# Tile 0's gate product computed among tile 1's expert rows, with its weights loaded twice

## The chip, the cores and the metric

The kernel runs on one core of a Trainium2 chip. The metric is the device time of one execution in microseconds (us). The engines are PE (TensorE), DVE (VectorE), ACT (ScalarE), POOL (GpSimd) and SP (SyncE, which here only issues weight loads); they run their own instruction lists and meet at semaphores.

## The reference, cut to what matters

Two layers follow one another on x of 256 tokens by 2048. The first ends with an expert lookup (each token takes 128 rows of `expert_u` and 128 rows of `expert_v`, each 2048 long) and a gated embedding; the second begins with a norm and a wide product.

```python
h = h + peer(rms_norm(h, ffn_norm_gain[i]), w_pq[i], sub_k1[i], sub_k2[i], expert_u[i], expert_v[i])
gate = jax.nn.sigmoid(rms_norm(h, ple_norm_gain[i]) @ w_ple_gate[i])
h = h + gate * (p[i] @ w_ple_proj[i])
...
h = rms_norm_2(x, norm_g)
proj = h @ w_in
```

The changed part is the line of `gate` and the sum behind it: a 256 x 2048 by 2048 x 2048 product, a sigmoid, and a sum into h.

## The kernel before, in words

Tokens lie in two tiles of 128 partitions (t = 0, 1); `h[:, t, :]` is the running sum. All large weights come as chunks of 128 x 2048 float32 (1 MiB): a chunk holds 512 rows of the weight by 512 columns, as four pieces k. A chunk c goes through five steps. SP loads it into one of the buffers `raw`. ACT's `split(c)` copies it to `whi` in a rounded format (signal `hi_done`). DVE's `split(c)` writes the rest, raw minus whi, to `wlo` (`lo_done`). PE multiplies: for each tile, eight products with `whi` (with the high part `xh` and the low part `xl` of the transposed input, four pieces each, signal `hi_used`) and four with `wlo` (`used`). `whi` and `wlo` have two buffers each, so ACT's copy of chunk c waits for `hi_used` and `lo_done` of chunk c-2, DVE's for `used` of c-2. SP loads c once `lo_done` of the chunk that had its `raw` buffer is there: two buffers while expert rows are gathered (`TWO_RAW`), four after.

`block_step` (L352) is one chunk's step on PE. Four chunks make a block of 512 output columns. The gate has 16 chunks (from `C_GATE`), four blocks n = 0 to 3.

Ahead of the gate are the expert rows. For pick i (0 to 127 belong to tile 0, 128 to 255 to tile 1), POOL gathers row u(i) and row v(i) for 128 tokens by an indirect DMA, 1 MiB each, in the order `ROW_ORDER`: u(i+8), then v(i). Eight or so buffers turn (`slots`; some lie in `xT`, in `raw` and in `whi`/`wlo`). DVE's `row_step` takes the dot product of u with the normed token, ACT makes a diagonal matrix of the weight, up to eight picks ahead of PE, and PE's loop over `PICKS` multiplies v by it (L774). In this loop stand also the second half of the query projection (chunks of its own, at picks 6 to 58), the embedding's projection (picks 86 and 92) and, for tile 0 alone, the turning of h into `xh`/`xl` (`gate_turn` on PE, `gate_entry` on ACT and DVE, at picks 160 to 188). Of tile 0's h nothing changes after DVE's pick 140 until the gate.

After the last row: DVE adds tile 1's sums into h (`peer_in`), PE turns tile 1, takes chunk 0 of the gate in parts (`gate_part`: tile 0 first, then tile 1), and then runs 15 `block_step`s with both tiles. The row norm is applied at the end, as the sigmoid's scale: ACT squares h's rows (`square_rows`, L984), DVE takes the mean, ACT the root (L988), DVE the reciprocal (`row_rstd`), and only then the first sigmoid (L1286) can run. Each block ends with ACT's sigmoids and DVE's product with `proj` and sum into h (L2043, L2046). In the last block the entry of the next norm (`entry(E_NORM2, ...)`, PE L396, ACT L975, DVE L1453) follows each chunk. The second layer's first stage, `in2_step`, comes next and uses both tiles. The order on each engine is written out by hand.

## Time and profile before

| | us |
|---|---|
| median of 3 runs (2412.11 to 2415.28) | 2414.21 |
| profiled execution, its own time | 2414.64 |
| its span | 2413.3 |
| granted TensorE clock, mean | 0.99 |
| PE busy | 2103.3 (87%) |
| DVE busy | 1402.8 (58%) |
| ACT busy | 650.9 (27%) |
| moved by DMA | 751.23 MB, mean 311 GB/s |

Times in all rows are us from the start of the span. Busy shares are averages over stages that have different limits, so a stage is read by itself: who is busy all of it, and what ended the waits of the others. In a row of the timeline, "x16" counts merged instructions, and the bracket at the end gives the idle time ahead of the group and who ended it.

### The profile page before, as it was taken

The numbers are of one execution on the slowest core, as the hardware profiler recorded it, in microseconds if no ns is written. First come the engines' busy times: TensorE is split into PE (matmuls) and PEld (weight loads), VectorE is DVE, ScalarE is ACT, GpSimd is POOL, SyncE is SP. The second block draws the span as 40 slices with busy tenths as digits, with TensorE's granted clock in tenths as the row PEclk, the third lists the DMA queues.
The fourth block names the chain that finished last, engine by engine and source line by source line (L and its number), as shares of the span: only waits on it lengthen the run. The fifth ranks groups of instructions, "written<-read, shape, count | busy, mean of one in ns | idle before, by whom it ended". The sixth has DMA issues, their size and how long they took to land.

```text
span 2413.3 us, 19575 instructions
## 1 busy us (share of the span) xinstructions
PE 2103.3 (87%) x7564; PEld 1348.0 (56%) x7564; DVE 1402.8 (58%) x1841; ACT 650.9 (27%) x923; POOL 666.7 (28%) x523
## 2 busy tenths in 40 slices
PE   8999979888887877777777777779999999999999
PEld 7887854444432433222332222227888888888887
DVE  4586685667586678444454444446557555744454
ACT  5464521111111110100010000005534443643332
POOL 0000144545455555554444444430000000000000
PEclk9999989999999999999999999999999999999999
DMA  7443489999999999999999999995455545455554
GB/s 285 158 173 124 157 340 420 413 422 421 421 421 421 421 422 414 422 421 421 422 422 421 421 422 421 421 407 222 175 208 179 198 174 175 160 195 194 189 180 147
DMA packets 105356, 751.23 MB, mean 311 GB/s; under 512 B 11952, under 2 KB 11952, under 8 KB 14384
## 3 DMA queue, kind: packets, MB, share of 16 engines
q0 software_dynamic: 73728, 536.90, 53.5%
q1 hardware_dynamic: 29520, 207.89, 23.9%
q10 hardware_dynamic: 2016, 5.18, 0.6%
q8 instruction: 60, 0.98, 0.2%
q14 instruction: 32, 0.26, 0.0%
HBM read 747.84 MB, written 2.10 MB: 311 GB/s over the span
## 4 chain that ended last, share of the span: by engine, by line
PE 56%; DMA 35%; DVE 4%; issue 2%; POOL 2%; ACT 1%; SPq 0%; ACTq 0%; POOLq 0%; DVEq 0%
PE ps L362 39%; DMA W<-in_expert_v,idx 26%; PE ps L774 12%; DMA raw<-in_expert_u,idx 3%; DMA wlo_row<-in_expert_v,idx 2%; DMA raw<-in_expert_v,idx 1%; DMA xT_rows<-in_expert_u,idx 1%; PE ps L396 1%; POOL W L313 1%; DMA W<-in_expert_u,idx 1%; DVE xT_rows L1854 1%; POOL xT_rows L313 0%; PE ps L662 0%; PE ps L661 0%; DVE raw L1854 0%
## 5 line engine op out<-in xcount | busy, mean ns | idle before, releaser
L362 PE MATMUL ps<-whi,xT 128*128 128x512 f32 x2560 | 616.2, 393 | 4.7 <-DVE xT L1453 2.0
L1442 DVE TENSOR_TENSOR wlo<-raw,whi 128x2048 fp32r<-128x2048 f32 x194 | 442.8, 2288 | 258.0 <-ACT whi L963 256.9
L774 PE MATMUL ps<-W 128*128 128x512 f32 x1008 | 465.3, 604 | 143.8 <-DMA W<-in_expert_v,idx 136.6
L362 PEld LDWEIGHTS ps<-whi,xT 128*128 128x128 f32 x2560 | 480.2, 189 | 105.7 <-DVE xT L1453 2.5
L963 ACT ACTIVATE whi<-raw 128x2048 fp32r<-128x2048 f32 x193 | 368.4, 1915 | 450.3 <-PE ps L362 256.6
L1854 DVE CUSTOM_DVE_ANT_0 W<-W 128x2048 f32<-128x2048 f32 x127 | 291.2, 2293 | 284.4 <-DMA W<-in_expert_u,idx 284.2
L774 PEld LDWEIGHTS ps<-W 128*128 128x128 f32 x1008 | 183.3, 191 | 415.3 <-issue 405.3
L362 PE MATMUL ps<-wlo,xT 128*128 128x512 f32 x1280 | 318.1, 391 | 7.4 <-DVE wlo L1442 7.4
L774 PE MATMUL ps<-raw,W 128*128 128x512 f32 x536 | 247.2, 604 | 71.0 <-DMA raw<-in_expert_v,idx 45.7
L362 PEld LDWEIGHTS ps<-wlo,xT 128*128 128x128 f32 x1280 | 241.3, 189 | 57.9 <-DVE wlo L1442 7.8
L313 POOL DMA_INDIRECT W<-in_expert_v,idx x129 | 185.1, 1435 | 259.9 <-PE ps L774 243.9
L1854 DVE CUSTOM_DVE_ANT_0 raw<-raw,W 128x2048 f32<-128x2048 f32 x68 | 155.8, 2291 | 144.3 <-DMA raw<-in_expert_u,idx 144.2
L1200 ACT ACTIVATE act<-act,st 128x8 f32<-128x8 f32 x32 | 9.6, 301 | 806.6 <-DVE act L1854 806.6
L774 PEld LDWEIGHTS ps<-raw,W 128*128 128x128 f32 x536 | 97.9, 191 | 213.0 <-issue 173.9
L774 PE MATMUL ps<-xT_rows,W 128*128 128x512 f32 x296 | 140.2, 620 | 43.9 <-DMA xT_rows<-in_expert_v,idx 26.4
L313 POOL DMA_INDIRECT W<-in_expert_u,idx x127 | 132.6, 1044 | 68.0 <-issue 36.0
L313 POOL DMA_INDIRECT raw<-in_expert_v,idx x68 | 97.4, 1432 | 143.5 <-PE ps L774 139.3
L774 PEld LDWEIGHTS ps<-xT_rows,W 128*128 128x128 f32 x296 | 55.8, 197 | 127.5 <-issue 103.7
L1246 ACT ACTIVATE W<-ident,act 128x128 f32<-128x128 f32 x256 | 80.5, 390 | 144.8 <-DVE act L1848 144.8
L1854 DVE CUSTOM_DVE_ANT_0 xT_rows<-xT_rows,W 128x2048 f32<-128x2048 f32 x37 | 84.5, 2290 | 53.7 <-DMA xT_rows<-in_expert_u,idx 53.5
L774 PE MATMUL ps<-wlo_row,W 128*128 128x512 f32 x176 | 83.9, 621 | 15.7 <-DMA wlo_row<-in_expert_v,idx 13.2
L319 POOL TENSOR_TENSOR W<-h,W 128x2048 f32<-128x2048 f32 x1 | 6.6, 6625 | 292.6 <-DVE st L1754 292.6
(317 smaller groups left out, 1708.2 us busy)
## 6 DMA issues: line engine op xcount, KB each, us to landing
raw<-in_weights SPq DMA_DIRECT2D x196, 1024.0 KB, 4.9
W<-in_expert_v,idx POOLq DMA_INDIRECT x129, 15.8
h<-in_x SPq DMA_DIRECT2D x8, 256.0 KB, 8.5
W<-in_expert_u,idx POOLq DMA_INDIRECT x127, 16.4
out<-h ACTq DMA_DIRECT2D x7, 256.0 KB, 2.6
raw<-in_expert_u,idx POOLq DMA_INDIRECT x68, 16.5
raw<-in_expert_v,idx POOLq DMA_INDIRECT x68, 11.0
W<-in_pool_op ACTq DMA_DIRECT2D x1, 1024.0 KB, 5.5
```

Of the source, the lines that this page charges most:

```text
L313: g.indirect_dma_start(dst, None, table[:, :], bass.IndirectOffsetOnAxis(idx[:, t, c:c + 1], 0)).then_inc(signal, 16)
L319: g.tensor_tensor(xn[:, 1, :], h[:, 1, :], ffn_row, ALU.mult).then_inc(sem["xn_ok"], 1)
L362: return pe.matmul(ps[:, (banks_of(b) if bank is None else bank) + t, 0:cols_n], x[:, q0 + qn * 4 + k, s], w_[:, cs], start=start, stop=stop)
L396: m = pe.transpose(ps[:, bank, (2 * k + t) * 128:(2 * k + t + 1) * 128], src(t, 2 * g + k), ident[:, :])
L774: m = pe.matmul(ps[:, (4 if t == 0 else 0) + b, :], diag[:, i % DIAGS, :], slots[SLOT_OF[n]][:, b * NC:(b + 1) * NC], start=(i % ROWS_OF_T ...
L963: a.activation(split_into(c)[0], raw[:, RAW_OF[c], :], ACT.Copy).then_inc(sem["hi_done"], 1)
L1200: a.activation(act[:, t, c:c + LAG], act[:, t, c:c + LAG], ACT.Gelu_apprx_tanh, scale=st[:, RSTD + t:RSTD + t + 1]).then_inc(sem["act_ok"], 1)
L1246: a.activation(diag[:, i % DIAGS, :], ident[:, :], ACT.Copy, scale=act[:, t, c:c + 1]).then_inc(sem["diag_ok"], 1)
L1442: v.tensor_tensor(lo, raw[:, RAW_OF[c], :], hi.bitcast(F32), ALU.subtract).then_inc(sem["lo_done"], 1)
L1854: v.tensor_tensor_reduce(slot, slot, xn[:, t, :], 1.0, 0.0, ALU.mult, ALU.add, act[:, t, c:c + 1]).then_inc(sem["u_used"], 1)
```

## The change

Tile 0's part of all 16 gate chunks is moved into the loop over the picks. The chunk numbers grow by 16: `C_TILE0` = 60 to 75 are the gate's chunks for tile 0, and `C_GATE` = 76 to 91 are the same weights, loaded a second time, for tile 1. Their buffers keep their turn. From pick `TILE0_AT` = 172 on, every fourth pick PE takes eight products of a chunk with `whi` (`tile0_hi`) and two picks later four with `wlo` (`tile0_lo`); ACT splits the chunk at its pick 169+4j, DVE at its pick 178+4j. The turning of tile 0 moves eight picks earlier. Tile 0's squares, mean and root are taken at picks 170 to 192. Sigmoids and sums into h of tile 0's blocks 0 to 2 run at ACT's picks 196, 212, 228 and DVE's 210, 226, 242. Of the last chunk (j = 15) PE's products stand behind the last row, and tile 0's last sigmoid and sum stand behind tile 1's entry. In the gate stage `block_step` gets `ts=(1,)`: tile 1 alone. Root and reciprocal are there taken for tile 1 alone.

```diff
@@ -69,10 +69,12 @@
...
 
-C_IN, C_ROPE, C_POOL, C_UQ, C_UKV, C_OUT, C_KEYS, C_PQ, C_PROJ, C_GATE, C_IN2, C_MERGE, C_OUT2, CHUNKS = (
-    0, 16, 17, 18, 21, 25, 41, 42, 58, 60, 76, 132, 180, 196)
+C_IN, C_ROPE, C_POOL, C_UQ, C_UKV, C_OUT, C_KEYS, C_PQ, C_PROJ, C_TILE0, C_GATE, C_IN2, C_MERGE, C_OUT2, CHUNKS = (
+    0, 16, 17, 18, 21, 25, 41, 42, 58, 60, 76, 92, 148, 196, 212)
 B_IN, B_ROPE, B_UQ, B_UKV, B_POOL, B_OUT, B_PQ, B_PROJ, B_GATE, B_IN2, B_MERGE, B_OUT2 = (
     0, 4, 5, 8, 12, 16, 20, 24, 28, 32, 46, 62)
+GATE_STEPS = C_GATE - C_TILE0
+TILE0_AT = 172
 TWO_RAW = range(C_PQ + 4, C_GATE + 2)
...
@@ -294,7 +296,7 @@
...
                         slot_left(sp, slot)
-                sp.dma_start(raw[:, RAW_OF[c], :], weights[c]).then_inc(landed[RAW_OF[c]], 16)
+                sp.dma_start(raw[:, RAW_OF[c], :], weights[c if c < C_GATE else c - GATE_STEPS]).then_inc(landed[RAW_OF[c]], 16)
             sp.wait_ge(sem["tile_out"], 2)
...
@@ -370,19 +372,19 @@
...
                         pe.wait_ge(sem["hi_done"], 1)
-                    for t in range(NT):
+                    for t in ts:
                         product(k, t, lh, hi, qn == 0 and k == 0, False)
...
                 if c == CHUNKS - 1:
-                    for t in range(NT):
+                    for t in ts:
                         for k in range(nk):
...
                 for k in range(nk):
-                    for t in range(NT):
+                    for t in ts:
                         m = product(k, t, lh, lo, False, qn == n_q - 1 and k == nk - 1)
...
@@ -714,26 +716,48 @@
...
 
-            def gate_part(t, part):
-                s = slice(t * 128, (t + 1) * 128)
+            def tile0_hi(j):
+                n, qn, c = j // 4, j % 4, C_TILE0 + j
+                hi = whi[:, BUF_OF[c], :]
+                if n == 0:
+                    pe.wait_ge(sem["turned_lo"], 8 * E_PLE + qn + 1)
+                if qn == 0 and n >= 2:
+                    pe.wait_ge(sem["gate0_out"], n - 1)
+                pe.wait_ge(sem["hi_done"], c + 1)
+                for k in range(4):
+                    cs = slice(k * NC, (k + 1) * NC)
+                    pe.matmul(ps[:, 5 - n % 2, :], xh[:, 4 * qn + k, 0:128], hi[:, cs], start=(qn == 0 and k == 0), stop=False)
+                    m = pe.matmul(ps[:, 5 - n % 2, :], xl[:, 4 * qn + k, 0:128], hi[:, cs], start=False, stop=False)
+                m.then_inc(sem["hi_used"], 1)
+
+            def tile0_lo(j):
+                n, qn, c = j // 4, j % 4, C_TILE0 + j
+                lo = wlo[:, BUF_OF[c], :]
+                pe.wait_ge(sem["lo_done"], c + 1)
+                for k in range(4):
+                    m = pe.matmul(ps[:, 5 - n % 2, :], xh[:, 4 * qn + k, 0:128], lo[:, k * NC:(k + 1) * NC], start=False, stop=(qn == 3 and k == 3))
+                m.then_inc(sem["used"], 1)
+
+            def gate_part(part):
                 hi, lo = whi[:, BUF_OF[C_GATE], :], wlo[:, BUF_OF[C_GATE], :]
-                pe.wait_ge(sem["turned_lo"], 8 * E_PLE + 4 * t + 1)
                 if part < 2:
                     if part == 0:
+                        pe.wait_ge(sem["gate0_out"], 3)
+                        pe.wait_ge(sem["turned_lo"], 8 * E_PLE + 5)
                         pe.wait_ge(sem["gate_hi"], 1)
...
                         cs = slice(k * NC, (k + 1) * NC)
-                        pe.matmul(ps[:, 4 + t, :], xh[:, k, s], hi[:, cs], start=(k == 0), stop=False)
-                        m = pe.matmul(ps[:, 4 + t, :], xl[:, k, s], hi[:, cs], start=False, stop=False)
+                        pe.matmul(ps[:, 5, :], xh[:, k, 128:256], hi[:, cs], start=(k == 0), stop=False)
+                        m = pe.matmul(ps[:, 5, :], xl[:, k, 128:256], hi[:, cs], start=False, stop=False)
                 else:
...
                             pe.wait_ge(sem["lo_done"], C_GATE + 1)
-                        m = pe.matmul(ps[:, 4 + t, :], xh[:, k, s], lo[:, k * NC:(k + 1) * NC], start=False, stop=False)
+                        m = pe.matmul(ps[:, 5, :], xh[:, k, 128:256], lo[:, k * NC:(k + 1) * NC], start=False, stop=False)
                 return m
...
@@ -784,30 +808,37 @@
...
                     proj_step((i - 86) // 6)
-                if i in (160, 164, 168, 172):
-                    if i == 160:
+                if i in range(TILE0_AT - 20, TILE0_AT - 4, 4):
+                    if i == TILE0_AT - 20:
                         pe.wait_ge(sem["peer_in"], 4)
-                    gate_turn(0, (i - 160) // 4)
-
+                    gate_turn(0, (i - TILE0_AT + 20) // 4)
+                j, rest = divmod(i - TILE0_AT, 4)
+                if 0 <= j < GATE_STEPS - 1:
+                    if rest == 0:
+                        tile0_hi(j)
+                    if rest == 2:
+                        tile0_lo(j)
+
+            tile0_hi(GATE_STEPS - 1)
             pe.wait_ge(sem["peer_in"], 7)
...
             gate_turn(1, 1)
-            for part in range(3):
-                gate_part(0, part)
-            gate_part(1, 0)
-            gate_part(1, 1).then_inc(sem["hi_used"], 1)
+            tile0_lo(GATE_STEPS - 1)
+            gate_part(0)
+            gate_part(1).then_inc(sem["hi_used"], 1)
             gate_turn(1, 2)
-            gate_part(1, 2).then_inc(sem["used"], 1)
+            gate_part(2).then_inc(sem["used"], 1)
             gate_turn(1, 3)
...
                         pe.wait_ge(sem["turned_lo"], 8 * E_PLE + 5 + qn)
-                    block_step(B_GATE + n, C_GATE + 4 * n + qn, qn, 4, bank=4 if n == 0 else None)
+                    block_step(B_GATE + n, C_GATE + 4 * n + qn, qn, 4, bank=4 if n == 0 else None, ts=(1,))
                     if n == 3 and qn in (1, 2, 3):
...
                             pe.wait_ge(sem["squared"], 6)
+                            pe.wait_ge(sem["emb0_ok"], 4)
                         pe.wait_ge(sem["emb_ok"], qn)
...
@@ -1215,6 +1246,14 @@
...
 
+            def tile0_sigmoid(n):
+                a.wait_ge(sem["used"], C_TILE0 + 4 * n + 4)
+                if n == 0:
+                    a.wait_ge(sem["rstd_ok"], 3)
+                else:
+                    a.wait_ge(sem["emb0_ok"], n)
+                a.activation(sg[:, 0, :], ps[:, 5 - n % 2, :], ACT.Sigmoid, scale=st[:, RSTD:RSTD + 1]).then_inc(sem["gate0_out"], 1)
+
             a.wait_ge(sem["first_mm"], 1)
...
@@ -1265,11 +1304,21 @@
...
                     proj_out((i - 91) // 6)
-                if i in (164, 168, 172, 176):
-                    if i == 164:
+                if i in range(TILE0_AT - 16, TILE0_AT, 4):
+                    if i == TILE0_AT - 16:
                         for slot in (4, 5, 6, 7):
                             slot_left(a, slot)
-                    gate_entry(0, (i - 164) // 4)
+                    gate_entry(0, (i - TILE0_AT + 16) // 4)
+                if i == TILE0_AT - 2:
+                    a.activation(xh[:, :, 128:256], h[:, 0, :].rearrange("p (k s) -> p k s", k=DK), ACT.Square,
+                                 accum_out=st[:, RSTD:RSTD + 1]).then_inc(sem["squared"], 1)
+                if i == TILE0_AT + 10:
+                    root(3, st[:, RSTD:RSTD + 1], "mean_ok", "root_ok")
+                j, rest = divmod(i - TILE0_AT + 3, 4)
+                if 0 <= j < GATE_STEPS and rest == 0:
+                    split(C_TILE0 + j)
+                if i in range(TILE0_AT + 24, TILE0_AT + 72, 16):
+                    tile0_sigmoid((i - TILE0_AT - 24) // 16)
 
...
@@ -1277,12 +1326,13 @@
...
             gate_entry(1, 3)
-
-            def sigmoids(b, last, sg_free, n):
+            tile0_sigmoid(3)
+
+            def sigmoids(b, last, sg_free, n, ts=range(NT)):
                 a.wait_ge(sem["used"], last + 1)
...
                     a.wait_ge(sg_free, n)
-                for t in range(NT):
+                for t in ts:
                     m = a.activation(sg[:, t, :], ps[:, (4 if b == B_GATE else banks_of(b)) + t, :], ACT.Sigmoid, scale=st[:, RSTD + t:RSTD + t + 1])
...
@@ -1292,15 +1342,14 @@
...
                     if n == 0 and qn == 1:
-                        square_rows(E_PLE, 0)
-                    if n == 0 and qn == 2:
+                        a.wait_ge(sem["turned_lo"], 8 * E_PLE + 8)
                         square_rows(E_PLE, 1)
                     if n == 0 and qn == 3:
-                        root(3, st[:, RSTD:RSTD + NT], "mean_ok", "root_ok")
-                        a.wait_ge(sem["rstd_ok"], 3)
+                        root(4, st[:, RSTD + 1:RSTD + 2], "mean_ok", "root_ok")
+                        a.wait_ge(sem["rstd_ok"], 4)
                     if n == 3 and qn:
                         entry(E_NORM2, qn - 1, c)
-                sigmoids(B_GATE + n, C_GATE + 4 * n + 3, sem["emb_ok"], n)
+                sigmoids(B_GATE + n, C_GATE + 4 * n + 3, sem["emb_ok"], n, ts=(1,))
 
...
@@ -1951,8 +2007,17 @@
...
                     split(C_PROJ + 1)
-                if i in (176, 180, 184, 188):
-                    gate_entry(0, (i - 176) // 4)
+                if i in range(TILE0_AT - 4, TILE0_AT + 12, 4):
+                    gate_entry(0, (i - TILE0_AT + 4) // 4)
+                if i == TILE0_AT + 12:
+                    row_mean(E_PLE, (0,))
+                if i == TILE0_AT + 20:
+                    row_scale(3, (0,))
+                j, rest = divmod(i - TILE0_AT - 6, 4)
+                if 0 <= j < GATE_STEPS and rest == 0:
+                    split(C_TILE0 + j)
+                if i in range(TILE0_AT + 38, TILE0_AT + 86, 16):
+                    tile0_emb((i - TILE0_AT - 38) // 16)
                 if i == 126:
...
@@ -1968,6 +2033,13 @@
...
                 m.then_inc(sem["turned_lo"], 1)
+
+            def tile0_emb(n):
+                cs = slice(n * NC, (n + 1) * NC)
+                v.wait_ge(sem["gate0_out"], n + 1)
+                own(v.tensor_tensor(sg[:, 0, :], sg[:, 0, :], proj[:, 0, cs], ALU.mult))
+                settled()
+                v.tensor_tensor(h[:, 0, cs], h[:, 0, cs], sg[:, 0, :], ALU.add).then_inc(sem["emb0_ok"], 1)
 
...
@@ -2029,29 +2101,27 @@
...
             gate_entry(1, 3)
+            tile0_emb(3)
             for n in range(4):
...
                     if n == 0 and qn == 3:
-                        row_rstd(E_PLE)
+                        row_rstd(E_PLE, 4, (1,))
                     if n == 3 and qn:
...
                 v.wait_ge(*evac_of(B_GATE + n))
-                for t in range(NT):
-                    own(v.tensor_tensor(sg[:, t, :], sg[:, t, :], proj[:, t, cs], ALU.mult))
-                settled()
-                for t in range(NT):
-                    m = v.tensor_tensor(h[:, t, cs], h[:, t, cs], sg[:, t, :], ALU.add)
-                m.then_inc(sem["emb_ok"], 1)
+                own(v.tensor_tensor(sg[:, 1, :], sg[:, 1, :], proj[:, 1, cs], ALU.mult))
+                settled()
+                v.tensor_tensor(h[:, 1, cs], h[:, 1, cs], sg[:, 1, :], ALU.add).then_inc(sem["emb_ok"], 1)
 
...
                 if i == 3:
-                    row_rstd(E_NORM2)
+                    row_rstd(E_NORM2, 5)
                 if i % 4 == 3:
...
```

What moves, on three engines. DVE among the rows of tile 1: names starting with W and raw are row buffers, `act` takes the dot products, L1854 and L1910 are the dot product, L1848 and L1904 the weights of eight rows. Before:

```order
L1854 ISA raw,act<-raw,W 128x2048
L1854 ISA act 128x1
L1848 TENSOR_TENSOR act<-act,gate 128x8
L1854 ISA W,act<-W 128x2048
L1854 ISA act 128x1
```

And with the change, in the same place:

```order
L1910 ISA raw,act<-raw,W 128x2048
L1910 ISA act 128x1
L1904 TENSOR_TENSOR act<-act,gate 128x8
L1910 ISA W,act<-W 128x2048
L1910 ISA act 128x1
L1910 ISA W,act<-W 128x2048
L1910 ISA act 128x1
L1491 TENSOR_TENSOR wlo<-raw,whi 128x2048
L2040 TENSOR_TENSOR tmp<-tmp,W 128x512
L2042 TENSOR_TENSOR h<-h,tmp 128x512
```

Once in four picks a subtraction of a chunk (L1491) comes in, and once in sixteen the product with `proj` and the sum into h.

ACT behind the last row, from the first copy behind tile 1's entry to the second block's first copy (`landed2` is the load's signal, `W,st<-h` the Square). Before:

```order
L963 ACTIVATE whi<-raw 128x2048 [waits lo_done,hi_used,landed2]
L984 ACTIVATE W,st<-h 128x2048 [waits turned_lo]
L963 ACTIVATE whi<-raw 128x2048 [waits lo_done,hi_used,landed3]
L984 ACTIVATE W,st<-h 128x2048 [waits squared]
L963 ACTIVATE whi<-raw 128x2048 [waits lo_done,hi_used,landed0]
L988 ACT_TABLE_LOAD
L988 ACTIVATE st<-st 128x2 [waits mean_ok]
L1286 ACT_TABLE_LOAD [waits used]
L1286 ACTIVATE tmp<-ps,st 128x512 [waits rstd_ok]
L1286 ACTIVATE tmp<-ps,st 128x512
L963 ACTIVATE whi<-raw 128x2048 [waits lo_done,hi_used,landed1]
```

With the change:

```order
L1255 ACT_TABLE_LOAD [waits emb0_ok]
L1255 ACTIVATE tmp<-ps,st 128x512 [waits used]
L994 ACTIVATE whi<-raw 128x2048 [waits lo_done,hi_used,landed2]
L1015 ACTIVATE W,st<-h 128x2048 [waits squared,turned_lo]
L994 ACTIVATE whi<-raw 128x2048 [waits lo_done,hi_used,landed3]
L994 ACTIVATE whi<-raw 128x2048 [waits lo_done,hi_used,landed0]
L1019 ACT_TABLE_LOAD
L1019 ACTIVATE st<-st 128x1 [waits mean_ok]
L1336 ACT_TABLE_LOAD [waits used]
L1336 ACTIVATE tmp<-ps,st 128x512 [waits rstd_ok]
L994 ACTIVATE whi<-raw 128x2048 [waits lo_done,hi_used,landed1]
```

A table load and tile 0's last sigmoid (L1255) now stand ahead of the first of these copies, one Square of two is gone, and one sigmoid of two.

PE in the last block of the gate stage, a chunk's hi and lo products with the entries of the next norm (`ident,h`) between them and the first step of the next stage. Before:

```order
L362 MATMUL ps<-wlo,xT 128x512 x8
L396 MATMUL ps<-ident,h 128x128 x8
L362 MATMUL ps<-whi,xT 128x512 x16
L362 MATMUL ps<-wlo,xT 128x512 x8
L396 MATMUL ps<-ident,h 128x128 x8
L362 MATMUL ps<-whi,xT 128x512 x16
```

With the change:

```order
L364 MATMUL ps<-wlo,xT 128x512 x4
L398 MATMUL ps<-ident,h 128x128 x8
L364 MATMUL ps<-whi,xT 128x512 x8
L364 MATMUL ps<-wlo,xT 128x512 x4
L398 MATMUL ps<-ident,h 128x128 x8
L364 MATMUL ps<-whi,xT 128x512 x16
```

The gate's steps have half as many products, the entries as many as before, and the next stage's step is whole again.

## Rows read from the trace of the kernel before

**Rows 1.** The page: chain of waits by engine; GB/s in 40 equal slices.
```profile
PE 56%; DMA 35%; DVE 4%; issue 2%; POOL 2%; ACT 1%; SPq 0%; ACTq 0%; POOLq 0%; DVEq 0%
...
GB/s 285 158 173 124 157 340 420 413 422 421 421 421 421 421 422 414 422 421 421 422 422 421 421 422 421 421 407 222 175 208 179 198 174 175 160 195 194 189 180 147
```

**Rows 2.** Stages: length, busy PE, PEld, DVE, ACT, POOL, PEclk, DMA share, GB/s.
```profile
1300.00:1600.00 300.00, 222.68 (x482) 87.25 (x483) 138.56 (x127) 19.22 (x63) 145.44 (x121) 0.99 1.01 422
...
1641.00:1720.00 79.00, 79.00 (x359) 65.53 (x358) 43.82 (x42) 40.48 (x39) 0.00 (x0) 1.00 0.56 202
```

**Rows 3.** DMA in 450 to 650: total, queues (packets, MB, share), weight loads (landing us).
```profile
DMA packets 11564, 84.28 MB, mean 421 GB/s; under 512 B 1281, under 2 KB 1281, under 8 KB 1281
...
q0 software_dynamic: 10549, 76.85, 92.4%
q1 hardware_dynamic: 1008, 7.34, 8.8%
...
raw<-in_weights SPq DMA_DIRECT2D x7, 1024.0 KB, 9.3
```

**Rows 4.** PE in order of time: start, length, operation, among the rows and in the gate.
```profile
1589.43 3.67 PE L774 MATMUL ps<-W 128*128 128x512 f32 x8 [1.29 <-DMA W<-in_expert_v,idx]
1594.41 3.67 PE L774 MATMUL ps<-raw,W 128*128 128x512 f32 x8 [1.31 <-DMA raw<-in_expert_v,idx]
...
1637.07 0.50 PE L728 MATMUL ps<-whi,xT 128*128 128x512 f32 x1
...
1640.76 3.91 PE L362 MATMUL ps<-whi,xT 128*128 128x512 f32 x16
...
1646.32 3.79 PE L362 MATMUL ps<-whi,xT 128*128 128x512 f32 x16
1649.95 1.98 PE L362 MATMUL ps<-wlo,xT 128*128 128x512 f32 x8
1651.76 3.79 PE L362 MATMUL ps<-whi,xT 128*128 128x512 f32 x16
...
1724.29 1.04 PE L396 MATMUL ps<-ident,h 128*128 128x128 f32 x8
1725.08 3.89 PE L362 MATMUL ps<-whi,xT 128*128 128x512 f32 x16
```

**Rows 5.** ACT in order of time in the gate stage.
```profile
1642.06 1.93 ACT L963 ACTIVATE whi<-raw 128x2048 fp32r<-128x2048 f32 x1
1643.86 1.93 ACT L984 ACTIVATE W<-h 128x2048 f32<-128x2048 f32 x1
...
1652.13 1.28 ACT L988 ACT_TABLE_LOAD   x1
...
1657.44 1.28 ACT L1286 ACT_TABLE_LOAD   x1 [2.69 <-PE ps L362]
1658.74 1.26 ACT L1286 ACTIVATE tmp<-ps,st 128x512 f32<-128x512 f32 x2
...
1712.30 1.57 ACT L975 ACTIVATE xT<-ps,colv 128x256 fp32r<-128x256 f32 x4 [5.78 <-PE ps L396]
```

**Rows 6.** DVE in order of time in the gate stage.
```profile
1644.02 2.29 DVE L1442 TENSOR_TENSOR wlo<-raw,whi 128x2048 fp32r<-128x2048 f32 x1 [0.68 <-ACT whi L963]
...
1660.11 1.29 DVE L2043 TENSOR_TENSOR tmp<-tmp,W 128x512 f32<-128x512 f32 x2 [5.15 <-ACT tmp L1286]
...
1713.17 1.66 DVE L1453 SCALAR_TENSOR_TENSOR xT<-ps,colv,xT 128x256 fp32r<-128x256 f32 x4 [3.92 <-ACT xT L975]
```

**Rows 7.** The page: DMA issues, count, KB each, median us to landing.
```profile
raw<-in_weights SPq DMA_DIRECT2D x196, 1024.0 KB, 4.9
W<-in_expert_v,idx POOLq DMA_INDIRECT x129, 15.8
...
raw<-in_expert_v,idx POOLq DMA_INDIRECT x68, 11.0
```

More of the change, by code:

```diff
@@ L116 @@
     "gelu_ok", "sgu_sq", "sgu_ok", "silu_b", "sgu_mm", "sgu_out", "sgu_gated", "sgu_T", "sgu_hi", "sgu_lo",
-    "merged_ok", "v_step", "first_half", "tile0_used", "tile_out", "gate_hi", "gate_lo",
+    "merged_ok", "v_step", "first_half", "tile0_used", "tile_out", "gate_hi", "gate_lo", "gate0_out", "emb0_ok",
     "load_x0", "load_x1", "load_x2", "load_x3", "load_cols", "load_rows", "load_pos", "load_pool_op", "load_p", "load_ffn", "load_ws", "load_out",
@@ L350, in matmul3, with block_step @@
                 return pe.matmul(o, a[1], b[0], start=False, stop=stop)
-            def block_step(b, c, qn, n_q, q0=0, cols_n=NC, lhs=None, bank=None, between=None):
+            def block_step(b, c, qn, n_q, q0=0, cols_n=NC, lhs=None, bank=None, between=None, ts=range(NT)):
                 lh, ll = lhs or (xh, xl)
@@ L1312, in in2_step @@
                 if i == 3:
-                    root(4, st[:, RSTD:RSTD + NT], "mean_ok", "root_ok")
+                    root(5, st[:, RSTD:RSTD + NT], "mean_ok", "root_ok")
             def group_squares(ap, signal):
@@ L1366, in merge_step @@
                 if i == 3:
-                    a.wait_ge(sem["rstd_ok"], 4)
+                    a.wait_ge(sem["rstd_ok"], 5)
                     sigmoids(b, c, sem["merged_ok"], 2 * n)
@@ L1455, in entry, with row_mean, row_scale, row_rstd @@
                     m.then_inc(sem["turned_lo"], 1)
-            def row_rstd(e):
-                ss = st[:, RSTD:RSTD + NT]
-                v.wait_ge(sem["squared"], 2 * e + 2)
+            def row_mean(e, ts):
+                ss = st[:, RSTD + ts[0]:RSTD + ts[-1] + 1]
+                v.wait_ge(sem["squared"], 2 * e + ts[-1] + 1)
                 v.tensor_scalar(ss, ss, 1.0 / D, EPS, ALU.mult, ALU.add).then_inc(sem["mean_ok"], 1)
-                v.wait_ge(sem["root_ok"], e + 1)
+            def row_scale(n, ts):
+                ss = st[:, RSTD + ts[0]:RSTD + ts[-1] + 1]
+                v.wait_ge(sem["root_ok"], n)
                 v.reciprocal(ss, ss).then_inc(sem["rstd_ok"], 1)
-                v.wait_ge(sem["rstd_ok"], e + 1)
+                v.wait_ge(sem["rstd_ok"], n)
+            def row_rstd(e, n, ts=range(NT)):
+                row_mean(e, ts)
+                row_scale(n, ts)
             def scaled_out(b, c, dst, scale, cols_n=NC):
@@ L1515, in vector_program @@
             split(4)
-            row_rstd(E_MIX)
+            row_rstd(E_MIX, 1)
             def pool_means(ks):
```

## The prediction

> **What bounds the kernel now.** I read the page's chain of waits and its slices first, then busy time by stage, then the DMA queues of two stretches, and last the engines in order of time around the gate. The chain is 56% PE and 35% DMA [rows 1]: two regimes that follow one another. In about 355 to 1630 us the expert rows are gathered; the slices stand at 413 to 422 GB/s there, and at 175 to 222 GB/s right after [rows 1]. By stage the DMA engines' share is 1.01 and the rate 422 GB/s in 1300 to 1600, with PE busy 74% and DVE 46%; in 1641 to 1720 PE is busy all 79 of 79 us with DMA at 0.56 [rows 2]. So a byte added among the rows costs time, and a product removed from the gate saves time as long as PE stays the one that is waited for. The change trades one for the other, and the question is how much of each is kept.
>
> **Bytes among the rows (the term that costs).** Sixteen chunks are loaded again. A chunk is 128 x 2048 x 4 bytes = 1.049 MB, sixteen are 16.78 MB. Does such a load fit beside the gathers? The trace has the case: in 450 to 650 seven weight chunks (7.34 MB on q1) were loaded while gathers ran, and the total is 84.28 MB in 200 us, 421.4 GB/s; q0 alone has 76.85 MB, 384 GB/s [rows 3]. In 1300 to 1600, with gathers only, it is 422 [rows 2]. The total stays and the gathers give way byte for byte. All sixteen are issued inside the stage (the first two when the projection's chunks leave their buffers, near row 86, the last near row 234 of 256). Cost: 16.78 MB / 421.4 GB/s = **39.8 us**. Bounds: 421.4 against 422 is at most 0.3 us in 200 us for seven chunks, so the upper end by such rows is about 41 us; the lower end, rows that had left the DMA engines free for some of it, is about 39 (the page's slices of 413 and 414, under 2% of 60 us each).
>
> **Everything else put among the rows is covered.** Per four picks (a u and a v row each, 4.97 us a pick from 1589.43 to 1594.41 [rows 4]) come one ACT copy (1.93 us [rows 5]), one DVE subtraction (2.29 [rows 6]) and twelve products (2.72, below). A window of four picks becomes 19.9 + 2.5 = 22.4 us; PE then works 4 x 3.67 [rows 4] + 2.7 = 17.4, DVE 4 x 2.3 + 2.3 = 11.6, ACT less. The Square, the root, three sigmoids and three sums into h are a few us over 80 picks. The new waits there: PE waits for hi_done and lo_done of each chunk, with the v rows queued behind and the gathers behind those; ACT waits for the landing, with the diagonals queued behind; DVE for used, with the dot products behind. By the picks at which each is placed they are met four or more picks, some 20 us, ahead (ACT copies at 169+4j what PE uses at 172+4j; DVE's subtraction at u row 178+4j stands near v row 170+4j, PE uses it at 174+4j); a landing took 9.3 us among rows [rows 3]. A gather is issued 11 to 16 us ahead of its landing [rows 7], so a short stop drains nothing. Cost taken: 0; if that cover were gone, the worst would be some us per chunk (a rival below).
>
> **Products taken out of the gate stage (the term that gains).** From PE's rows [rows 4]: a step of a chunk for both tiles takes 1646.32 to 1651.76 = 5.44 (the first, from 1640.76, 5.56), of which the sixteen hi products are 3.63 and the eight lo products 1.81; for one tile it is 2.72 (eight hi 1.81, four lo 0.91). Before, the stage from chunk 1's step to the first step of the next stage is 1640.76 to 1725.08 = 84.3 us. At PE's own pace it would be 15 x 2.72 + 3 entries x 0.8 (1724.29 to 1725.08) = 43.2, a gain of 41.1. But the copies and subtractions per chunk don't halve, and they chain. I follow the chain on the clock of before:
>
> Start: PE gets to chunk 1's step at 1640.76 as before. Out go tile 0's twelve products of chunk 0 (2.9 us up to 1637.07), in come chunk 15's twelve products of tile 0 (2.7 us), and what PE meets at 1637.07 is DVE's entry of tile 1, which starts only after chunk 0's subtraction. Neither a gain nor a loss there, within 0.5 us.
>
> Chunk 2: before, ACT copies it at 1642.06 [rows 5]. Now tile 0's last sigmoid stands ahead: table load 1.28 and half of 1.26 [rows 5]; copy from 1643.95 to 1645.9, subtraction to 1648.2, PE's last product 1649.1. Chunk 3: ACT has one Square (1.9 [rows 5]) ahead, copy to 1649.65, subtraction to 1651.95, PE done 1652.9. PE has by then idled 4 us.
>
> The root: ACT copies chunk 4 to 1651.5, loads the root's table to 1652.8, DVE subtracts chunk 4 to 1654.2 and gives the mean, root at 1654.4, the sigmoid's table load to 1655.85, sigmoid (one tile, half of a pair's 1.26) to 1656.45; the sum into h behind it (two operations, half of 1.29 each [rows 6]) ends before chunk 5's subtraction. Before, the same chain ends at 1660 [rows 5] and is hidden behind PE's steps; now the copy of chunk 5 waits behind it: to 1658.4, subtraction to 1660.7. PE finishes chunk 5 at 1661.7, chunks 6 and 7 at its pace: T = 1667.1.
>
> A steady block of four (from one block's last product, T): sigmoid T+0.2 to T+0.8, copy of the second chunk to T+2.7, subtraction to T+5.0, its lo products to T+6.0, two more chunks 5.44: 11.45 instead of 10.9. T = 1678.55.
>
> The last block has three entries of 0.8 on PE, and ACT's and DVE's parts of them (1.57 and 1.66 [rows 5, 6]): chunk 13 done T+6.0, entry 6.8, chunk 14 9.5, entry 10.3, chunk 15's hi 12.1, but its subtraction only at 12.4 (ACT: entry to 8.2, copy to 10.1; DVE to 12.4), lo 13.4, entry 14.2. The next stage starts at 1678.55 + 14.2 = 1692.75, and its first steps use both tiles again and find what they found before. **Gain: 1725.08 - 1692.75 = 32.3 us.** Landings hold: a chunk's buffer is free about 9 us before its copy, a landing alone takes 4.9 [rows 7], and the stage then moves a chunk per 3.5 us, 303 GB/s, under the 422 seen.
>
> A table load is weighed apart. The row shows 1.28 us with the ACTIVATE 0.02 us behind it, at 1657.44 and 1658.74 [rows 5], and there are three on the stage's chain now (before two). The Trainium skill, page "ScalarE: Activation LUTs", section "What ACT_TABLE_LOAD costs", gives a load and a drain of about 1.38 us, 2.66 us together; with it the stage would lose about 4 us more and the sum would be 2426. The trace doesn't show the drain, so the row's price stands.
>
> **Sum.** Profiled execution before: 2414.64 us, span 2413.3, median of the runs 2414.21, so the two agree within 0.5. 2414.6 + 39.8 - 32.3 = **2422.1**, 0.3% slower.
>
> **Rivals.**
> - Gate at PE's pace (no difference to be seen): if the chained copies overlap better than by my hand, up to 41.1 us come back: 2414.6 + 39.8 - 41.1 = 2413.3. For it: DVE needs only 2.3 us a chunk against PE's 2.72. Against it: the root and the sigmoids stand in ACT's order ahead of copies, and that order doesn't change. Below 2419 needs over 3 us of it.
> - The bytes ride along (faster): the limit of 422 could be that of the gathers' own queue, and a second queue would come on top; then the stage costs 0 to 10 us and the time is 2382 to 2392. It decides in my disfavour once the added bytes cost under 27.6 us (32.3 less the 0.2% of 4.8). Against it: q0 fell to 384 while q1 carried 36.7, with an unchanged total [rows 3], and the engines' share is 1.01 [rows 2].
> - The row pipeline stalls: one of the new in-order waits is met late and the gathers run dry, 1 to 2 us a chunk, 16 to 32 us: 2438 to 2454. For it: nine waits per chunk on three engines which feed each other in a ring. Against it: the 20 us ahead, and that 450 to 650 holds its rate with the same kind of waits.
> - Each added load pays its latency: alone a chunk lands in 4.9 us [rows 7], 2.4 more than its bytes at 422; unhidden, sixteen make 38 us, 2460. In 450 to 650 seven of them cost nothing of the sort. The page "DMA: Bandwidth & Descriptors" of the Trainium skill, section "Anatomy of one DMA — SWDGE (gpsimd) path", puts a fixed part of about 2.0 us on each transfer, which is this rule; the trace agrees for a lone load and not for one among gathers.
>
> **How the numbers follow.** 0.2% (4.8 us; 2409.4 to 2419.0) is about what a measurement of this kernel tells from no change. Forecast 2419 to 2428: 0.68. Gate nearer PE's pace, 2411 to 2419: 0.17. Bytes ride along: 0.05. Row stalls, 2428 up: 0.08. Latency unhidden: 0.02. Faster 0.05, same 0.17, slower 0.78. The range takes the forecast, most of the PE-pace case and the first part of the stalls: 2415 to 2430.
>
> **What would show it.** In the profile after: the DMA queues of the whole run hold 768 MB instead of 751.23; the rows stage ends near 1670 instead of 1630, with 421 to 422 GB/s in tile 1's rows. PE's full steps in the gate are eight and four products, with idle time that names ACT's copy, largest ahead of chunk 5 (3 us or more); from chunk 1's step to the next stage's first it is 52 us. A rows stage that grew by well under 39 us, or a rate over 422, shows the second rival; PE waiting for whi or wlo among the rows with the rate falling shows the third; a gate stage under 47 us shows the first.

## The result, and the profile after

The changed kernel takes 2423.45 us (median of 6 runs, 2420.86 to 2425.61) against 2413.8 before (6 runs, 2411.12 to 2415.28): ratio 1.004, 95% interval 1.003 to 1.005, 9.65 us slower. 2422.1 was predicted. Its profiled execution took 2423.82 us with a span of 2422.4.

On the page of the changed kernel, the total of the DMA and its queues (packets, MB, share of 16 engines):

```profile
DMA packets 107661, 768.01 MB, mean 317 GB/s; under 512 B 12208, under 2 KB 12208, under 8 KB 14640
...
q0 software_dynamic: 73728, 536.90, 53.4%
q1 hardware_dynamic: 31824, 224.67, 25.6%
```

768.01 MB are the 751.23 of before and the sixteen chunks. By stage (length, busy PE, PEld, DVE, ACT, POOL with counts, PEclk, DMA share, GB/s), three stretches, two among tile 1's rows and one in the gate:

```profile
1300.00:1400.00 100.00, 80.93 (x195) 37.96 (x193) 50.87 (x43) 16.46 (x26) 45.29 (x37) 0.93 1.01 421
1400.00:1500.00 100.00, 83.27 (x194) 39.72 (x195) 51.46 (x46) 20.36 (x33) 42.87 (x36) 0.90 1.01 421
...
1682.00:1735.00 53.00, 47.78 (x210) 37.35 (x209) 43.89 (x42) 41.27 (x40) 0.00 (x0) 0.97 0.84 304
```

Among the rows the DMA share and the rate are those of [rows 2], with PE busier (81 to 83% for 74%). In the gate PE is no longer busy all the time (47.78 of 53.00; in [rows 2] 79.00 of 79.00), and DVE and ACT are busy 83% and 78% of it. PE in order of time, from the last v row to the next stage's first step (start, length, operation, count, idle time ahead and who ended it):

```profile
1671.66 1.95 PE L798 MATMUL ps<-W 128*128 128x512 f32 x4 [1.18 <-DMA W<-in_expert_v,idx]
...
1681.99 2.08 PE L364 MATMUL ps<-whi,xT 128*128 128x512 f32 x8
1683.92 1.07 PE L364 MATMUL ps<-wlo,xT 128*128 128x512 f32 x4
1687.36 3.19 PE L364 MATMUL ps<-whi,xT 128*128 128x512 f32 x8 [2.38 <-ACT whi L994]
...
1699.58 2.11 PE L364 MATMUL ps<-whi,xT 128*128 128x512 f32 x8 [2.20 <-ACT whi L994]
1701.91 1.19 PE L364 MATMUL ps<-wlo,xT 128*128 128x512 f32 x4 [0.21 <-DVE wlo L1491]
...
1708.40 1.98 PE L364 MATMUL ps<-whi,xT 128*128 128x512 f32 x8
...
1719.96 1.98 PE L364 MATMUL ps<-whi,xT 128*128 128x512 f32 x8
...
1734.37 3.89 PE L364 MATMUL ps<-whi,xT 128*128 128x512 f32 x16
```

Chunk 1's step starts at 1681.99 and the next stage at 1734.37: 52.4 us, where [rows 4] have 84.3. The first four-chunk part ends at 1708.40 (26.4 us), the next block takes 11.56, the last 14.41. The two stops of over 2 us wait for ACT's copies of chunk 2 and chunk 5. ACT at the second of them:

```profile
1689.01 3.70 ACT L994 ACTIVATE whi<-raw 128x2048 fp32r<-128x2048 f32 x2
1692.73 1.28 ACT L1019 ACT_TABLE_LOAD   x1
1695.53 0.20 ACT L1019 ACTIVATE st<-st 128x1 f32<-128x1 f32 x1 [1.52 <-DVE st L1509]
1695.75 1.28 ACT L1336 ACT_TABLE_LOAD   x1
1697.04 0.69 ACT L1336 ACTIVATE tmp<-ps,st 128x512 f32<-128x512 f32 x1
1697.63 3.71 ACT L994 ACTIVATE whi<-raw 128x2048 fp32r<-128x2048 f32 x2
```

It is the chain of the prediction: table load, wait for DVE's mean, root, table load, sigmoid, and only then the copy that PE waits for. In [rows 5] the same chain stands behind chunk 4's copy too, and PE doesn't notice it.

In what follows three times of each kernel's profiled execution are compared: the start of the last v row's products, of chunk 1's step, and of the next stage's first step. Each row is one execution. Where the rows stage begins differs between them by some us too (below, at run 3), so differences of the first column carry an error of that size; those of the last don't.

| kernel | last v row | chunk 1 | next stage | gate, from chunk 1 |
|---|---|---|---|---|
| before | 1630.42 | 1640.76 | 1725.08 | 84.3 |
| the change | 1671.66 | 1681.99 | 1734.37 | 52.4 |
| change without its loads | 1631.45 | 1641.79 | 1694.17 | 52.4 |
| before with the loads | 1671.05 | 1681.38 | 1765.69 | 84.3 |
| change, gate reordered | 1668.51 | 1678.83 | 1726.02 | 47.2 |
| blocks 0 and 1 only | 1650.31 | 1660.64 | 1734.18 | 73.5 |
| blocks 2 and 3 only | 1649.61 | 1662.41 | 1727.85 | 65.4 |

### The profile page after: what moved, and what is told of

It is laid out like the page before. It is cut to its first block, busy times and chain, and to the rows that moved or that the text cites. A ratio compares the mean times of both kernels' runs of the same rounds, so it can differ in the third digit from the quotient of the medians.

```text
span 2422.4 us, 19674 instructions
## 1 busy us (share of the span) xinstructions
PE 2127.3 (88%) x7564; PEld 1361.4 (56%) x7564; DVE 1438.1 (59%) x1859; ACT 692.4 (29%) x949; POOL 680.1 (28%) x523
## 2 busy tenths in 40 slices
DMA packets 107661, 768.01 MB, mean 317 GB/s; under 512 B 12208, under 2 KB 12208, under 8 KB 14640
## 4 chain that ended last, share of the span: by engine, by line
PE 53%; DMA 35%; DVE 5%; issue 3%; POOL 2%; ACT 1%; SPq 0%; ACTq 0%; POOLq 0%; DVEq 0%
PE ps L364 37%; DMA W<-in_expert_v,idx 14%; DMA raw<-in_expert_v,idx 12%; PE ps L798 11%; DMA raw<-in_expert_u,idx 4%; DMA wlo_row<-in_expert_v,idx 3%; DMA xT_rows<-in_expert_u,idx 2%; POOL W L315 1%; PE ps L398 1%; DMA W<-in_expert_u,idx 1%; DVE wlo L1491 1%; DVE xT_rows L1910 1%; DVE raw L1910 1%; DVE W L1910 1%; POOL xT_rows L315 1%
## 5 line engine op out<-in xcount | busy, mean ns | idle before, releaser
L1491 DVE TENSOR_TENSOR wlo<-raw,whi 128x2048 fp32r<-128x2048 f32 x210 | 479.0, 2287 | 247.2 <-ACT whi L994 246.1
L364 PE MATMUL ps<-whi,xT 128*128 128x512 f32 x2440 | 590.1, 394 | 9.2 <-ACT whi L994 5.9
L994 ACT ACTIVATE whi<-raw 128x2048 fp32r<-128x2048 f32 x209 | 398.5, 1913 | 467.5 <-PE ps L364 245.0
L364 PEld LDWEIGHTS ps<-whi,xT 128*128 128x128 f32 x2440 | 457.7, 189 | 106.9 <-issue 4.9
L1910 DVE CUSTOM_DVE_ANT_0 W<-W 128x2048 f32<-128x2048 f32 x127 | 291.0, 2291 | 258.0 <-DMA W<-in_expert_u,idx 257.8
L798 PE MATMUL ps<-raw,W 128*128 128x512 f32 x536 | 274.4, 660 | 103.2 <-DMA raw<-in_expert_v,idx 86.8
L364 PE MATMUL ps<-wlo,xT 128*128 128x512 f32 x1220 | 305.6, 392 | 8.0 <-DVE wlo L1491 8.0
L364 PEld LDWEIGHTS ps<-wlo,xT 128*128 128x128 f32 x1220 | 230.3, 189 | 57.9 <-DVE wlo L1491 10.1
L798 PEld LDWEIGHTS ps<-raw,W 128*128 128x128 f32 x536 | 108.0, 210 | 262.0 <-issue 205.8
L1910 DVE CUSTOM_DVE_ANT_0 raw<-raw,W 128x2048 f32<-128x2048 f32 x68 | 156.2, 2297 | 166.3 <-DMA raw<-in_expert_u,idx 166.2
L315 POOL DMA_INDIRECT W<-in_expert_v,idx x129 | 178.0, 1380 | 225.7 <-PE ps L798 202.4
L315 POOL DMA_INDIRECT W<-in_expert_u,idx x127 | 158.2, 1246 | 67.7 <-issue 36.0
L1910 DVE CUSTOM_DVE_ANT_0 xT_rows<-xT_rows,W 128x2048 f32<-128x2048 f32 x37 | 84.5, 2289 | 58.5 <-DMA xT_rows<-in_expert_u,idx 58.3
```

Of the source, the lines that this page charges most:

```text
L315: g.indirect_dma_start(dst, None, table[:, :], bass.IndirectOffsetOnAxis(idx[:, t, c:c + 1], 0)).then_inc(signal, 16)
L364: return pe.matmul(ps[:, (banks_of(b) if bank is None else bank) + t, 0:cols_n], x[:, q0 + qn * 4 + k, s], w_[:, cs], start=start, stop=stop)
L798: m = pe.matmul(ps[:, (4 if t == 0 else 0) + b, :], diag[:, i % DIAGS, :], slots[SLOT_OF[n]][:, b * NC:(b + 1) * NC], start=(i % ROWS_OF_T ...
L994: a.activation(split_into(c)[0], raw[:, RAW_OF[c], :], ACT.Copy).then_inc(sem["hi_done"], 1)
L1491: v.tensor_tensor(lo, raw[:, RAW_OF[c], :], hi.bitcast(F32), ALU.subtract).then_inc(sem["lo_done"], 1)
L1910: v.tensor_tensor_reduce(slot, slot, xn[:, t, :], 1.0, 0.0, ALU.mult, ALU.add, act[:, t, c:c + 1]).then_inc(sem["u_used"], 1)
```

## The experiments

**1. Who pays for the 41 us among the rows: the bytes or the work?** Two runs take the change apart. The first is the change without its sixteen loads:

```diff
-RAW_ROUND = [RAW_OF[:c + 1].count(RAW_OF[c]) for c in range(CHUNKS)]
+NOT_LOADED = range(C_TILE0, C_GATE)
+RAW_ROUND = [sum(RAW_OF[b] == RAW_OF[c] and b not in NOT_LOADED for b in range(c + 1)) for c in range(CHUNKS)]
...
+                if c in NOT_LOADED:
+                    continue
                 sp.dma_start(raw[:, RAW_OF[c], :], weights[c if c < C_GATE else c - GATE_STEPS]).then_inc(landed[RAW_OF[c]], 16)
```

> The changed kernel without its sixteen added loads: copies, subtractions, products, sigmoids and sums of tile 0 stay among the rows and work on whatever the raw buffers hold, so tile 0's gate is not computed from its weights. Theory (the rows stage pays for bytes alone, 16.78 MB at 421.4 GB/s): 39.8 us less than the changed kernel's 2423.5, 2383.7, that is 30 us faster than before, with the gate stage unchanged at 52.4 us from chunk 1's step to the next stage. Rival (part of the 41 us that the rows stage grew is the new work and its in-order waits): 2390 or more.

It takes 2383.29 us (4 runs, 2381.88 to 2385.13; ratio to before 0.9875, 0.986 to 0.989): 30.3 us under before, 40.2 under the change. With all copies, subtractions and products of tile 0 still among the rows, the last v row comes at 1631.45, 1.0 us after that of before. The new work and its in-order waits cost nothing there that can be told from the spread of executions. The waits for the added chunks' landings are not in this run; the sum at the end of run 2 covers them.

**2. The loads alone.** The kernel before with sixteen loads that nobody reads. The first two start at 768 us as in the change; the others start some eight picks earlier than there (the third at 1192.0 us, in the change at 1233.4), all of them among the rows:

```diff
                 if c == C_GATE:
+                    for j in range(16):
+                        if j < 2:
+                            sp.wait_ge(sem["lo_done"], C_PROJ + j + 1)
+                        else:
+                            sp.wait_ge(sem[f"extra{j % 2}"], 16 * (j // 2))
+                            sp.wait_ge(sem["u_used"], 170 + 4 * (j - 2) + 1)
+                        sp.dma_start(raw[:, (j + 1) % 2, :], weights[C_GATE + j]).then_inc(sem[f"extra{j % 2}"], 16)
...
                     row_landed(sp, NEAR_END)
```

> The kernel before with sixteen more weight loads of 1 MiB among the rows, at the same picks, used by nobody. Theory (bytes alone): 2413.8 + 39.8 = 2453.6. Rival (loads ride along unless ACT and DVE wait for them, or each pays its latency of 4.9 us): 2414 to 2440, or 2490.

It takes 2454.29 us (4 runs, 2450.66 to 2457.91; ratio 1.0168, 1.0152 to 1.0184), 40.7 over the 2413.61 beside it. Its DMA in 1200 to 1600:

```profile
DMA packets 23162, 168.60 MB, mean 422 GB/s; under 512 B 2587, under 2 KB 2587, under 8 KB 2587
...
q0 software_dynamic: 21264, 154.85, 93.0%
q1 hardware_dynamic: 1889, 13.64, 8.2%
...
raw<-in_weights SPq DMA_DIRECT2D x13, 1024.0 KB, 9.1
```

The total is the 422 GB/s of [rows 2] and q1's 13.64 MB are missing from q0. The two halves add up: -30.3 for the work without loads, +40.7 for the loads without work, together +10.4 where the change has +9.65. The bytes are paid in full, and of a load's own latency (9.1 us from issue to landing here, 4.9 alone) hardly anything is paid: 0.9 us for all sixteen. As the sum isn't under the change's own +9.65, nothing is left for late waits on the landings either, which neither half has.

**3. What keeps 9 us of the gain?** The change with another order on ACT and DVE in the gate. On ACT (DVE's sums into h move in the same way, its mean stands one subtraction earlier, and ACT's Square one copy later):

```diff
-            tile0_sigmoid(3)
...
+                    if n == 1 and qn == 1:
                         a.wait_ge(sem["rstd_ok"], 4)
+                        sigmoids(B_GATE, C_GATE + 3, sem["emb_ok"], 0, ts=(1,))
+                        tile0_sigmoid(3)
+                    if n > 1 and qn == 0:
+                        sigmoids(B_GATE + n - 1, C_GATE + 4 * n - 1, sem["emb_ok"], n - 1, ts=(1,))
-                sigmoids(B_GATE + n, C_GATE + 4 * n + 3, sem["emb_ok"], n, ts=(1,))
+            sigmoids(B_GATE + 3, C_GATE + 15, sem["emb_ok"], 3, ts=(1,))
```

> The changed kernel with ACT's and DVE's order in the gate stage changed: each block's sigmoid and sum stand behind the copy and subtraction of the next block's second chunk (in the first block behind the third chunk's), tile 0's last sigmoid and sum share the first sigmoid's table load, and the row mean is taken one subtraction earlier. Theory (the 9 us between the gate's 52.4 us and PE's own pace of 43.2 are the serial chain of root, table loads, sigmoid and copy): by the durations of the trace the stage falls to about 46 us, so 2423.5 - 6.3 = 2417. Rival (the stage is held by DVE's subtractions, by weight landings or by the lower clock seen there): within 2 us of 2423.5.

It takes 2415.66 us (11 runs, 2414.56 to 2424.8; ratio 1.0017, 1.0006 to 1.0028): 7.8 under the change, 2.1 over before. The gate takes 47.2 us instead of 52.4 (46 expected). ACT where the stops were:

```profile
1687.57 1.28 ACT L1019 ACT_TABLE_LOAD   x1
1688.87 0.20 ACT L1019 ACTIVATE st<-st 128x1 f32<-128x1 f32 x1
1688.98 3.71 ACT L994 ACTIVATE whi<-raw 128x2048 fp32r<-128x2048 f32 x2
1692.70 1.28 ACT L1335 ACT_TABLE_LOAD   x1
1694.00 0.69 ACT L1335 ACTIVATE tmp<-ps,st 128x512 f32<-128x512 f32 x1
```

The root now waits for nobody, and two copies stand between it and the sigmoid. PE's largest stops in this gate are 0.36 and 1.13 us; the steady blocks run at 2.72 a chunk. So the serial order was the cause of these 5.2 us, and not DVE's throughput or the landings. The run moves several things at once (tile 0's sigmoid ahead of chunk 2, the Square, the root, each block's sigmoid), and doesn't say what each is worth.

The two profiled executions are 8.4 us apart, of which only 5.2 are the gate's. The other 3.2 show in the last v row (1668.51 for 1671.66), but 2.7 of them are there before the rows begin, in a part that nobody changed. The step of PE just ahead of the rows, in the change and in this run:

```profile
345.73 3.78 PE L364 MATMUL ps<-wlo,xT 128*128 128x512 f32 x8 [7.37 <-DVE wlo L1491]
343.06 3.58 PE L364 MATMUL ps<-wlo,xT 128*128 128x512 f32 x8 [7.37 <-DVE wlo L1495]
```

In the kernel before it starts at 345.52, in the loads alone at 348.52. What makes executions differ there is open. So only the 5.2 us can be put down to the new order.

**4. Half of the change, early.** Only blocks 0 and 1 are moved (eight chunks, eight added loads):

```diff
-    0, 16, 17, 18, 21, 25, 41, 42, 58, 60, 76, 92, 148, 196, 212)
+    0, 16, 17, 18, 21, 25, 41, 42, 58, 60, 68, 84, 140, 188, 204)
...
-                    block_step(B_GATE + n, C_GATE + 4 * n + qn, qn, 4, bank=4 if n == 0 else None, ts=(1,))
+                    block_step(B_GATE + n, C_GATE + 4 * n + qn, qn, 4, bank=4 if n == 0 else None, ts=(1,) if n < 2 else range(NT))
```

> Half of the change: only the gate's first eight chunks (blocks 0 and 1) are taken for tile 0 among the rows and loaded twice; blocks 2 and 3 run with both tiles as before. Theory: the loads cost 8 x 1.049 MB / 421.4 GB/s = 19.9 us; from chunk 1's step to chunk 7's end the stage takes 26.4 us instead of 38.2, a gain of 11.8; sum 2413.8 + 8.1 = 2421.9, nearly the whole loss for half of the change, because the chain of the first block is lost once. Rival (each chunk moved loses the same): half of 9.65, 2418.6.

It takes 2423.87 us (5 runs, 2420.27 to 2425.77; ratio 1.0043, 1.0029 to 1.0056): half of the change loses 10.3 us, no less than the whole. The last v row is 19.9 us later than before, what the eight loads should cost; the gate gains 10.8, a little under the 11.8 expected, for which PE has a row:

```profile
1666.01 2.06 PE L364 MATMUL ps<-whi,xT 128*128 128x512 f32 x8 [2.38 <-ACT whi L994]
...
1678.23 3.63 PE L364 MATMUL ps<-whi,xT 128*128 128x512 f32 x8 [2.37 <-ACT whi L994]
...
1688.07 3.79 PE L364 MATMUL ps<-whi,xT 128*128 128x512 f32 x16
```

The same two stops, and behind the second eight products take 3.63 instead of 2.0: the granted clock was 0.53 in 1678 to 1680 (last section). From chunk 5's step to chunk 8's it is 9.8 us (1678.23 to 1688.07), in the change 8.8 (1699.58 to 1708.40): that is the missing 1.0. The loss doesn't go with the number of chunks; it belongs to the stops in the gate's first six chunks.

**5. Half of the change, late.** Blocks 2 and 3 instead; the same count of loads and of products, but the root's chain falls among whole steps. Tile 0's last sigmoid, which stood with its table load ahead of chunk 2's copy, is then also gone from the gate:

```diff
-                sp.dma_start(raw[:, RAW_OF[c], :], weights[c if c < C_GATE else c - GATE_STEPS]).then_inc(landed[RAW_OF[c]], 16)
+                sp.dma_start(raw[:, RAW_OF[c], :], weights[c if c < C_TILE0 else c + GATE_STEPS if c < C_GATE else c - GATE_STEPS]).then_inc(landed[RAW_OF[c]], 16)
...
-                    block_step(B_GATE + n, C_GATE + 4 * n + qn, qn, 4, bank=4 if n == 0 else None, ts=(1,))
+                    block_step(B_GATE + n, C_GATE + 4 * n + qn, qn, 4, bank=4 if n == 0 else None, ts=range(NT) if n < 2 else (1,))
```

> The other half of the change: only the gate's last eight chunks (blocks 2 and 3) are taken for tile 0 among the rows and loaded twice; blocks 0 and 1 run with both tiles as before, and ACT's and DVE's order is the written one. It adds the same eight loads and takes out the same 96 products as the first half did. Theory (the loss is the root's chain, which PE's steps hide while they have both tiles): loads +19.9 us; up to chunk 7 the stage takes what it took before, then a block of 11.6 and a last block of 14.4 stand for 46.1 us, a gain of 20.1. Sum 2413.6 - 0.2 = 2413.4, no change against before, 10 us under the first half. Rival (what counts is the number of chunks moved): the first half's 2423.9, or half of the whole change's loss, 2418.5.

It takes 2417.47 us (11 runs, 2414.26 to 2420.28) beside 2415.37 of before in the same set: ratio 1.0011, 1.0002 to 1.002, 2.1 us slower where -0.2 was expected. Each against its own kernel before, the two halves are 8.2 us apart (10 expected), in the sense expected; the root's chain and tile 0's sigmoid are hidden or gone together, and the run doesn't part them. The theory missed 2.3 us, and the trace gives two places. PE:

```profile
1649.61 2.78 PE L800 MATMUL ps<-W 128*128 128x512 f32 x4 [2.17 <-DMA W<-in_expert_v,idx]
1653.17 1.97 PE L716 MATMUL ps<-ident,h 128*128 128x128 f32 x8 [0.78 <-DVE h L1917]
...
1703.92 2.11 PE L364 MATMUL ps<-whi,xT 128*128 128x512 f32 x8 [0.44 <-ACT whi L996]
1706.97 1.20 PE L364 MATMUL ps<-wlo,xT 128*128 128x512 f32 x4 [0.94 <-DVE wlo L1494]
```

The gate takes 65.4 us, not 64.2: the first one-tile block follows a block that still has two sigmoids and two sums, and I had counted one of each (12.85 us for it, not 11.6). The other 2.5 us stand ahead of chunk 1: from the last v row to chunk 1's step it is 12.8 us, in all others 10.3. In this execution TensorE's granted clock was 0.70 in 1649 to 1653, with the last v row's products, and 0.56 in 1653 to 1658, where PE turns tile 1 and begins with chunk 0. Whether that is so in most executions of this kernel one profile doesn't tell.

No version that loads what it uses is faster than the kernel before. A chunk moved costs 2.49 us of bytes and can give back at most PE's 2.72; over sixteen chunks that leaves, by the sum's own bound, 41.1 - 39.8 = 1.3 us, and the reordered kernel is still 4 us of chain away from it.

## Why the prediction was right

By its steps, against the trace of the changed kernel:

- **Bytes among the rows, 39.8.** Last v row 41.2 later here; 40.6 with the loads alone, 38.1 in the reordered kernel, 19.9 and 19.2 with eight loads. The three with sixteen average 40.0; single executions lie up to 2 us off. The term rests better on the medians: 40.7 us for the loads alone and 40.2 less without them. In this execution 555 to 655 ran at 413 GB/s, ahead of the first added load at 768, and up to 1150, with two added loads issued, it had moved 0.4 MB less than the kernel before in the same time: 1 us of the 41.2 that isn't the added bytes'. (The prediction puts the slices of the rows at 413 to 422; the last whole one in [rows 1] is 407. Nothing hangs on it.)
- **All other work among the rows, 0.** Held: 1.0 us without the loads, and the change's last v row is only 0.6 later than that of the loads alone. The cover named (each wait met some 20 us ahead) was enough.
- **Start of the gate, 0 within 0.5.** From the last v row to chunk 1's step 10.33 us, before 10.34.
- **The chain in the gate.** First part 26.3 predicted and 26.4 measured, steady block 11.45 and 11.55, last block 14.2 and 14.4; in all 52.0 and 52.4, gain 32.3 and 31.9. One sign of the prediction failed: the stop ahead of chunk 5 was to be the largest, "3 us or more"; it is 2.20, and the largest is the 2.38 ahead of chunk 2. By the count's own times it was 2.8 (chunk 4 done at 1655.6, chunk 5's copy at 1658.4). The total doesn't feel this, for it follows the copies on ACT and not where PE stands idle: from chunk 1's step to chunk 5's it is 17.6 us, and 17.6 in the count. This hand count is worth more than the two easy ones: PE's pace alone gives 43.2 us and 2413.3, no difference; halving the stage gives 42.
- **Table loads.** Three in the gate, 1.28 us each. In the rows of the changed kernel the root's table load ends at 1694.0 while ACT waits for DVE, and the sigmoid's, 1695.75 to 1697.03, has its ACTIVATE 0.01 behind it. The Trainium skill's 2.66 us for a switch (page "ScalarE: Activation LUTs", section "What ACT_TABLE_LOAD costs") isn't to be seen at either.
- **The sum.** 39.8 - 32.3 = +7.5 predicted, 41.2 - 31.9 = +9.3 in the two profiled executions (span 2422.4 less 2413.3 is 9.1), +9.65 in the medians. Of the 1.8 us between the first two, 1.4 are the rows' term and 0.4 the gate's. That 2422.1 lies only 1.35 from the measured 2423.45 is partly luck: it stands on the profiled execution's 2414.6, 0.8 above the median of 2413.8, so the change itself was forecast 2.15 us too small.

Of the rivals, "gate at PE's pace" is what the reordered kernel comes near to; "bytes ride along", "row pipeline stalls" and "latency unhidden" are each ruled out by runs 1 and 2. The last would have cost 38 us over the bytes, and run 2 shows 40.7 - 39.8 = 0.9. The Trainium skill, "DMA: Bandwidth & Descriptors", section "Anatomy of one DMA — SWDGE (gpsimd) path", gives some 2.0 us fixed per transfer, for transfers that GpSimd issues; these are SyncE's. Paid sixteen times that would be 32 us, an estimate from the page's figure, and run 2 doesn't show them.

## What to carry to other kernels

Where a stage runs at the DMA engines' full rate, price what is moved into it by its bytes alone, however idle the other engines are, and compare that with what the engine that is relieved really gives back. Halving one engine's work in a stage doesn't halve the stage: follow by hand the order in which the engines beside it feed it, and look above all for chains (mean, root, table load, sigmoid) that were free only because the long steps hid them. Here the chain belonged to the first blocks, and moving half of the work lost as much as moving all.
